# Moving the matmul operands H, Y and G from place 64 to place 192, modulo 512 bytes, relative to the weights in SBUF

## What is computed

```python
p = h @ a_in[i]                                   # 1024 x 2560
x = x + jnp.concatenate([y_main, y_mem], axis=-1) @ w_o[i]
x = x + (jax.nn.silu(h @ w_gate) * (h @ w_up)) @ w_down   # 1024 x 2816 twice, 2816 x 1024
kv = rmsnorm(x, kv_norm) @ w_kv_shared            # 1024 x 1536
z = h @ w_in                                      # 1024 x 7200, block three
merged = jax.nn.sigmoid(ga) * (a @ w_br_a) + jax.nn.sigmoid(gb) * (ob @ w_br_b)
```

## Time and profile before

| | kernel before |
|---|---|
| median of 3 runs | 1132.66 us (1132.13 to 1133.08) |
| the profiled execution | 1128.94 us |
| its span, first to last instruction | 1127.6 us |
| PE busy | 1103.6 us, 98% of the span |
| PEld busy | 1064.1 us, 94% |
| DVE busy | 831.3 us, 74% |
| ACT busy | 631.2 us, 56% |
| POOL busy | 146.6 us, 13% |
| DMA | 221.49 MB, mean 196 GB/s |

### The profile page before, as it was taken

How to read it: one execution, slowest core, us unless ns; L and a number is a source line. 1 busy time by engine, 2 the same in 40 slices (tenths; PEclk the granted TensorE clock), 3 DMA queues, 4 the chain that set the end, 5 groups by cost and what they waited for, 6 DMA issues and landing times.

```text
span 1127.6 us, 21751 instructions
## 1 busy us (share of the span) xinstructions
PE 1103.6 (98%) x8926; PEld 1064.1 (94%) x8926; DVE 831.3 (74%) x1307; ACT 631.2 (56%) x954; POOL 146.6 (13%) x109
## 2 busy tenths in 40 slices
PE   8999999999999999999999999999999998999997
PEld 6989999999988899999999898989999997999996
DVE  5767688888876767777777678398556889767766
ACT  5655654434665655444444675576547466555554
POOL 0002201000000003110001000000001034444441
PEclk9999999999999999999999999999999999999999
DMA  9655578776644345788888745344435553656651
GB/s 342 217 166 171 183 241 282 247 254 209 202 138 149 131 128 191 230 295 277 281 263 293 248 158 196 115 158 167 162 113 175 198 181 133 194 187 187 187 169 38
DMA packets 60610, 221.49 MB, mean 196 GB/s; under 512 B 6752, under 2 KB 7008, under 8 KB 60128
## 3 DMA queue, kind: packets, MB, share of 16 engines
q1 hardware_dynamic: 60048, 218.53, 59.2%
q10 hardware_dynamic: 288, 1.05, 0.3%
q0 software_dynamic: 176, 0.52, 0.1%
HBM read 219.03 MB, written 1.05 MB: 195 GB/s over the span
## 4 chain that ended last, share of the span: by engine, by line
PE 84%; DVE 10%; ACT 3%; issue 2%; DMA 1%; SPq 0%; ACTq 0%; DVEq 0%
PE PS L388 24%; PE PS L389 24%; PE PS L390 23%; PE PS L393 13%; DVE w_lo L1453 3%; ACT w_hi L914 2%; DVE PS L2101 1%; DVE ARENA L1486 1%; DMA ARENA<-memT 1%; DVE SQ L1486 0%; DVE SQ L1761 0%; DVE H_lo L1496 0%; DVE SQ L1468 0%; DVE Y_lo L1492 0%; PE PS L494 0%
## 5 line engine op out<-in xcount | busy, mean ns | idle before, releaser
L1453 DVE TENSOR_TENSOR w_lo<-raw,w_hi 128x1024 fp32r<-128x1024 f32 x324 | 396.7, 1227 | 156.0 <-ACT w_hi L914 155.1
L914 ACT ACTIVATE w_hi<-raw 128x1024 fp32r<-128x1024 f32 x356 | 371.7, 1054 | 119.3 <-PE PS L390 93.5
L388 PE MATMUL PS<-Y_hi,w_hi 128*128 128x256 f32 x1208 | 340.1, 282 | 5.4 <-ACT GF L1411 1.7
L389 PE MATMUL PS<-Y_lo,w_hi 128*128 128x256 f32 x1208 | 337.3, 279 | 0.0
L390 PE MATMUL PS<-Y_hi,w_lo 128*128 128x256 f32 x1208 | 337.1, 279 | 0.0
L388 PEld LDWEIGHTS PS<-Y_hi,w_hi 128*128 128x128 f32 x1208 | 226.7, 188 | 8.7 <-ACT GF L1411 1.9
L389 PEld LDWEIGHTS PS<-Y_lo,w_hi 128*128 128x128 f32 x1208 | 226.9, 188 | 0.5 <-issue 0.2
L390 PEld LDWEIGHTS PS<-Y_hi,w_lo 128*128 128x128 f32 x1208 | 226.3, 187 | 0.0
L388 PE MATMUL PS<-H_hi,w_hi 128*128 128x256 f32 x768 | 216.7, 282 | 1.7 <-DVE w_lo L1453 0.9
L389 PE MATMUL PS<-H_lo,w_hi 128*128 128x256 f32 x768 | 214.1, 279 | 0.0
L390 PE MATMUL PS<-H_hi,w_lo 128*128 128x256 f32 x768 | 213.8, 278 | 0.0
(11 more groups left out here) (258 smaller groups left out, 1391.5 us busy)
## 6 DMA issues: line engine op xcount, KB each, us to landing
raw<-stream SPq DMA_DIRECT2D x404, 512.0 KB, 4.2
ARENA<-memT SPq DMA_DIRECT2D x2, 512.0 KB, 7.4
X<-xT SPq DMA_DIRECT2D x1, 1024.0 KB, 11.0
ARENA<-ctxT SPq DMA_DIRECT2D x1, 1024.0 KB, 6.5
ARENA<-memT SPq DMA_DIRECT2D x1, 1024.0 KB, 8.1
outT<-ARENA SPq DMA_DIRECT2D x4, 256.0 KB, 2.6
CROW<-c_rows SPq DMA_DIRECT2D x1, 512.0 KB, 10.7
ARENA<-c_rows SPq DMA_DIRECT2D x1, 512.0 KB, 12.0
```

The source lines that it names most:

```text
L388: pe.matmul(o, wh, xh, start=start, stop=False, skip_group_check=True)
L389: pe.matmul(o, wh, xl, start=False, stop=False, skip_group_check=True)
L914: act.activation(w_hi[n % RING][:], raw[at][:], ACT.Copy).then_inc(*mark("hi", n))
L1453: dve.tensor_tensor(w_lo[n % RING][:], raw[raw_of("slot", n)][:], w_hi[n % RING][:], ALU.subtract).then_inc(*mark("lo_dve", n))
```

## The change

The change moves memory only. The two pads go. V (400 floats a partition, 1600 bytes), GS (24 floats, 96 bytes) and EPS_COL (one float, which takes 32 bytes) are allocated ahead of H in place of the pad of 64 bytes. No instruction is added, removed, reordered or resized.

```diff
-HALF_LINE = 16
...
         X = sb("X", [P, KC, T])
-        sb("phase", [P, HALF_LINE])
+        V = sb("V", [P, VEC_N])
+        GS = sb("GS", [P, 3, KC])
+        EPS_COL = sb("EPS_COL", [P, 1])[:]
         H = (sb("H_hi", [P, KC, T], F32R), sb("H_lo", [P, KC, T], F32R))
         Y = (sb("Y_hi", [P, KC, T], F32R), sb("Y_lo", [P, KC, T], F32R))
         G = [(sb(f"G_hi{i}", [P, T], F32R), sb(f"G_lo{i}", [P, T], F32R)) for i in range(2)]
-        sb("whole", [P, HALF_LINE])
         SQ = sb("SQ", [P, KC, T])
...
         scan_m = sb("scan_m", [P, T])
-        V = sb("V", [P, VEC_N])
         MOD = sb("MOD", [P, NMOD, 2])
-        GS = sb("GS", [P, 3, KC])
         CROW = sb("CROW", [P, D])
-        EPS_COL = sb("EPS_COL", [P, 1])[:]
         small = sb("small", [P, 64])
```

## The result

The kernel after takes 1118.15 us (median of 4 runs, 1111.42 to 1121.81) against 1132.87 us before (4 runs, 1132.13 to 1133.58): ratio 0.9864, 95% interval 0.9845 to 0.9882. It is faster, and inside the range, but short of the forecast of 1105.8 by 12 us, where the rival "partly" stood (1119). The runs spread over 10 us, those of before over 1.5. That small spread is in part the luck of four: 43 further runs of the kernel before, taken beside the experiments, go from 1124.48 to 1135.16 us. One more, at a granted clock of 0.75, took 1346.57 us and is left out.

The account below looks back on a forecast made before the run. TensorE's matmul spacing bounds the kernel: 24.3 us (dense tall slots) + 3.6 (early and mid projections) + 0.9 (wide, HP) - 2.0 (DVE) = 26.8, from 1128.94 to 1102.1; the median, 3.7 higher, is 1105.8 us. Range 1100 to 1138.

Parts of the forecast that it names:

- the rival "partly": Tall slots: place 192 has both paces but is fast more often, say half of the slow slots; 1119 us, chance 0.13.
- What bounds the kernel, and that place counts: Whole kernel: TensorE, busy 98%, sets the time, and the operands' relative place affects its matmul spacing; other engines gain nothing.
- 0.107 us a slot: Tall slots: gain of each slow slot that turns fast, 24 matmuls by 4.44 ns.
- The rule of the Trainium skill: TensorE: independent read ports, so loading weights takes no bandwidth from the running matmul; place can't matter, sum 0.
- 192 is three times as far from 0 as 64 is: Tall slots with H, Y, G: moving from 64 to 192 leads away from the slow case, so all at 113.3 ns.
- d: All matmuls: the moving operand's place less the stationary one's; in tall H, Y, G slots from 64 to 192.
- the second meeting: Tall matmuls: an extra 4.6 ns when d is so near 0 that the streams also meet at the seam between matmuls.
- the first of the signs of being wrong: Matmul starts: two paces still, with other slots fast.
- Meetings of 4.6 ns each: All matmuls: time above the base is one to four meetings of the moving stream and weight load, some 4.6 ns each.
- I take 2 us off: ffn0 slots with modulation work: with PE faster, DVE's `w_lo` comes late now and then; 2 us lost.
- DVE's 83%: ffn0: DVE's busy share, 144 of 180 us before, becomes 83% with PE 3.8% faster.
- Wide and HP slots: Wide matmuls with Y gain up to 1.0 us, HP matmuls up to 0.7 us; half of both, 0.9 us.

Follow-up runs that it names:

- 1 to 3: Kernel after, ARENA back at 448: 1115.62 us; kernel before, all but H, Y, G moved: 1133.74 us; kernel before, 192 bytes ahead of everything: 1131.08 us.
- 4: Small kernel of TensorE alone, tall matmuls, moving operand at 16 places in steps of 32 bytes: 113.3 to 120.0 ns a matmul.
- 10: TensorE alone, own or next weights 112 bytes from the moving operand: 116.7 and 118.3 ns; of 27 more places, only 112 at 113.3 ns.
- 11: TensorE alone, places 0, 64, 112 and 192 with fewer loaded columns or other moving lengths: 113.3 to 120.0 ns for 32 x 256, about 111.7 for 128 x 128.
- 9: H, Y and G in one tensor at place 112, other tensors at their places of the kernel before: 1109.99 us, ratio 0.9802.

## Why the prediction was partly right

**What bounds the kernel, and that place counts: right.** PE's spacing set the time, through the relative place of H, Y and G (1 to 3), between the same 113.3 and 117.8 ns, and DVE, ACT, POOL and the DMAs were indifferent to theirs. 0.107 us a slot is the right price: ffn1 at place 112 gave 6.8 us for 66 slots. The rule of the Trainium skill ("TensorE: Matmul & The Clock Gate", Part 2) that the two read ports are independent and that a load takes nothing from the running matmul, which spoke for no change, isn't borne out for these float32r matmuls: with nothing else running, the distance of 256 columns goes from 113.3 to 123.3 ns by place alone (4 and 10), and it also changes with the number of columns loaded (11).

**The step that failed: "192 is three times as far from 0 as 64 is, ... so the trend over d leads away from the second meeting."** I had three values of d and drew a line over a circle of 512. The circle has 256 bytes, 64 and 448 differ there (64 and 192), and the map isn't monotone: 96 and 128 are worse than 64. At 192 a break can leave either pace, and 183 of 318 slots came out fast: the rival "partly", to which I gave 0.13, and the first of the signs of being wrong that I named. Its price was right, 14 us against 14.7. That the time still fell inside my range is the width of the range, not the mechanism. The rows of before had the hint: CX at 448 was fast in 3 of its 5 tall slots, and that is the very relation that the change gives to H, Y and G. I read "both paces occur" at 64 and at 448 as the same case, and didn't count how often each.

**Meetings of 4.6 ns each: not borne out.** The sizes in 11 show some steps of about 4.5 ns (113.3 to 117.8, 228.8 to 233.3), but with places and load widths that the picture of two streams and a seam doesn't order, and the pairs in 10 don't fit it.

**"I take 2 us off" for DVE: the place was right, the size was not.** `w_lo` did come late at the slots with modulation work. But I took it for a delay now and then, and it is a limit: the round trip DVE, ACT, DVE takes 8.38 us for three slots, the fast pace needs 8.16. DVE's 83% was right too, (8.38 - 1.44)/8.38; what it hides is that the other 17% are waits inside that round trip, which PE's pace can't shorten. With the fast pace kept (9), ffn0 loses 5.5 us of 7.1: 3.3 more in waits for `w_lo`, 1.6 in half clock behind one of them, 0.7 back from `G_lo`, and the rest in the slow distances behind each late start. I had not counted the clock at all.

**Wide and HP slots: 0.9 us expected, nothing net.** Y's 240 wide matmuls of 512 gained 4.1 ns each, as hoped; CX's 96 lost as much, and the 256-column ones lost 4.1 to 4.5 in five slots of six. HP came down 1.6 ns, not 7.

Why 19.1 us at place 112, not 26.8 (profiled executions): 3.5 are ffn0's excess over the 2 us, 0.9 the wide slots', 1.5 the other stages that I took as dense (ffn1, ffn2, w_o0, w_o1, r, ga and gb gave 15.8 for 17.3), and the rest, about 1.9, the early and mid projections, where two thirds of a slot's gain was too much to count.

## What to carry over

When a stream of matmuls misses its expected spacing by a few per cent, look at the starts, count which share of the restarts is fast, and sweep the moving operand's relative place in a small kernel of matmuls alone before moving memory in a large one: two values of a periodic thing give no trend. A spread of runs that comes from nowhere (1111 to 1122 us) can be an undecided pace inside the program; a layout that decides it (1109 to 1112 us) is worth more than the median of the spread. And when the bounding engine gets faster, compare its new pace with the period of the round trips that feed it, not with their busy share, and look at its clock behind each new standstill.

## What was not expected of the hardware

- float32r matmuls of 256 columns with loads of 128 have a pace that depends on the place of the moving operand relative to the stationary one, modulo 256 bytes: 113.3 at 112 only, 113.3 or 117.8 at 192, 117.8 at 64, 120.0 at 0 and 96, 115.6 to 123.3 at the odd multiples of 4, mostly 120 and more. Over the whole kernel that is 1109.99 to 1147.81 us.
- A pace, once caught, holds for hundreds of matmuls, and a single distance of 0.25 us can lose it. At 112 it comes back by itself within about ten matmuls.
- With 128 columns moving the distance is 111.7 ns at all four places tried: hardly less than the 113.3 for twice as many.
- A standstill of PE of 2.02 us in an otherwise dense stage was followed by 17 matmuls at half clock (213 ns). One of 1.26 us, 11 us before, was not, and neither was one of 2.01 us in the kernel before (at 304.80 us). So length alone doesn't decide it.
- A `w_lo` subtraction on DVE takes 1.22 us, and 2.6 where it begins while the same one runs on POOL; where DVE's begins first, POOL's takes 2.6 to 2.9 us in place of 2.4.
- Why 112, and what the 4.5 ns are, stays open.
